# Two more PSUM banks for the last projection panel, and a group's elementwise work moved from GpSimd to VectorE and ScalarE

## The reference, cut to what matters

```python
xbc = silu(causal_depthwise_conv(xbc, conv_w, conv_b))     # 4 taps along the sequence, on x, B and C
y = ssd_chunked_scan(xs * dt, dt * a, bm, cm)              # a scan over chunks, state carried
y = y + d_skip * xs
y = y * silu(z)                                            # the gating
y = rmsnorm(y, norm_g)                                     # needs the sum of y*y over all groups
x = x + y @ w_out
```

## Time and profile before

| | |
|---|---|
| median of 3 runs | 2429.52 us (2429.28 to 2430.1) |
| span of the profiled execution | 2427.2 us |
| the profiled execution's time outside its span | not recorded |
| PE busy | 2237.2 us (92%) |
| DVE busy | 1369.1 us (56%) |
| ACT busy | 709.5 us (29%) |
| POOL busy | 215.7 us (9%) |
| mean granted TensorE clock | 0.961 of full speed |

### The profile page before, as it was taken

How to read it: one execution, slowest core, us unless ns; L and a number is a source line. 1 busy time by engine, 2 the same in 40 slices (tenths; PEclk the granted TensorE clock), 3 DMA queues, 4 the chain that set the end, 5 groups by cost and what they waited for, 6 DMA issues and landing times.

```text
span 2427.2 us, 27940 instructions
## 1 busy us (share of the span) xinstructions
PE 2237.2 (92%) x9790; PEld 1764.4 (73%) x9790; DVE 1369.1 (56%) x2135; ACT 709.5 (29%) x907; POOL 215.7 (9%) x196
## 2 busy tenths in 40 slices
PE   4999989898998989899889999799999987887999
PEld 3888778686876867687678888678877766564887
DVE  4466766767676676767863323352257773445333
ACT  4222122222212222221433212252234453433211
POOL 0000301102030120203000000000000101111000
PEclk9999999999999999999999999999999998988999
DMA  4645454453545445353444323613332221100432
GB/s 139 199 142 168 122 162 143 133 157 113 162 128 153 140 139 148 124 157 127 165 159 159 124 95 130 214 56 95 94 90 82 84 66 52 37 7 22 143 129 86
DMA packets 213887, 294.19 MB, mean 121 GB/s; under 512 B 16122, under 2 KB 150162, under 8 KB 212690
## 3 DMA queue, kind: packets, MB, share of 16 engines
q1 hardware_dynamic: 200946, 256.18, 33.8%
q0 software_dynamic: 8624, 29.04, 4.6%
q10 hardware_dynamic: 4272, 8.39, 0.9%
HBM read 273.51 MB, written 20.05 MB: 121 GB/s over the span
## 4 chain that ended last, share of the span: by engine, by line
PE 82%; DVE 9%; issue 7%; ACT 1%; DMA 0%; POOL 0%; DVEq 0%; SPq 0%; ACTq 0%; POOLq 0%
PE ps L1878 24%; PE ps L1879 23%; PE ps L1880 23%; PE ps L1948 2%; DVE w_lo L1186 2%; PE ps L2145 1%; PE ps L1952 1%; DVE xst L1279 1%; PE ps L1955 1%; PE ps L2126 1%; DVE bct L1279 1%; PE ps L2124 1%; PE ps L1962 1%; PE ps L1939 1%; PE ps L2074 1%
## 5 line engine op out<-in xcount | busy, mean ns | idle before, releaser
L1878 PE MATMUL ps<-hn_hi,w_hi 128*128 128x512 f32 (+1 forms) x1296 | 538.2, 415 | 67.9 <-DVE gz L1298 45.4
L1880 PE MATMUL ps<-hn_hi,w_lo 128*128 128x512 f32 (+1 forms) x1296 | 518.4, 400 | 0.0
L1879 PE MATMUL ps<-hn_lo,w_hi 128*128 128x512 f32 (+1 forms) x1296 | 518.3, 400 | 0.0
L1414 DVE TENSOR_TENSOR w_lo<-w_raw,w_hi 128x1024 fp32r<-128x1024 f32 x178 | 217.7, 1224 | 531.8 <-ACT w_hi L945 530.5
L1186 DVE TENSOR_TENSOR w_lo<-w_raw,w_hi 128x1024 fp32r<-128x1024 f32 (+1 forms) x166 | 206.5, 1246 | 302.6 <-ACT w_hi L858 301.8
L945 ACT ACTIVATE w_hi<-w_raw 128x1024 fp32r<-128x1024 f32 x178 | 188.4, 1059 | 550.6 <-PE ps L1880 523.0
L1878 PEld LDWEIGHTS ps<-hn_hi,w_hi 128*128 128x128 f32 (+1 forms) x1296 | 247.1, 191 | 139.7 <-DVE w_lo L1186 76.4
L858 ACT ACTIVATE w_hi<-w_raw 128x1024 fp32r<-128x1024 f32 (+1 forms) x166 | 172.5, 1041 | 542.1 <-PE ps L1880 535.0
L1878 PE MATMUL ps<-w_hi,y_hi 128*128 128x512 f32 x768 | 307.1, 400 | 9.1 <-DVE y_lo L1423 6.1
L1879 PE MATMUL ps<-w_lo,y_hi 128*128 128x512 f32 x768 | 305.7, 398 | 0.0
L1880 PE MATMUL ps<-w_hi,y_lo 128*128 128x512 f32 x768 | 305.6, 398 | 0.0
(11 more groups left out here) (323 smaller groups left out, 2416.0 us busy)
## 6 DMA issues: line engine op xcount, KB each, us to landing
ada_raw<-in_w_ada_dram SPq DMA_DIRECT2D x128, 384.0 KB, 3.4
w_raw<-in_ssm_w_in_dram SPq DMA_DIRECT2D x96, 512.0 KB, 4.5
w_raw<-in_ssm_w_in_dram SPq DMA_DIRECT2D x128, 256.0 KB, 3.5
w_raw<-in_w_in_dram SPq DMA_DIRECT2D x64, 512.0 KB, 3.8
w_raw<-in_ssm_w_out_dram SPq DMA_DIRECT2D x60, 512.0 KB, 3.7
csb<-cs_rows POOLq DMA_DIRECT2D x32, 512.0 KB, 5.9
w_raw<-in_w_out_dram SPq DMA_DIRECT2D x32, 512.0 KB, 5.5
y_rows<-yt POOLq DMA_DIRECT2D x8, 1024.0 KB, 4.7
```

The lines of the kernel that those rows point to most:

```text
L1414: nc.vector.tensor_tensor(w_lo[:, slot, :], w_raw[:, slot, :], w_hi[:, slot, :].bitcast(F32), ALU.subtract).then_inc(lo_ready, 1)
L1878: nc.tensor.matmul(out_, a_hi, b_hi, start=start, stop=False)
L1879: nc.tensor.matmul(out_, a_hi, b_lo, start=False, stop=False)
L1880: return nc.tensor.matmul(out_, a_lo, b_hi, start=False, stop=stop)
```

## The change

- Panel 4 goes to banks 6 and 7, and its gate is taken in one piece. PE now waits, at u = 16, until the scan has left these banks (`y_chunk_skipped`); at u = 0 for the copy of panel 2, made at u = 13; at u = 4 for the gate of panel 3; and, ahead of the scan's first `chunk_sum`, for the gate of panel 4.
- DVE multiplies each chunk by `gz` right behind `chunk_skip` (five instructions there now, four before). POOL does no arithmetic in the groups, and stores `yt` ahead of `ada_part`.
- The first tap of each convolution is an ACT instruction (`conv_tap`, six for each group), the six others stay on DVE.
- ACT squares the gated chunk (`y_squares`, u = 17, three instructions into the scan's free buffers), DVE adds them up (`y_add`, four instructions at u = 18 and 19, in two sums `ysq` and `ysq_b`).
- The convolutions start one step earlier (u = 14, 16, 17), their constants at u = 12, and `ada_rows` take the steps of `ADA_SLOTS`, with its loads one step later on SP.
- Some semaphores of the second block are merged; no wait changes there.

```diff
+Z_BANK = (2, 6)
+ADA_SLOTS = (*range(1, 14), 15, 18, 19)
@@ SP
-                    k = u - AHEAD
+                    k = u - AHEAD - ADA_SLOTS[0]
@@ POOL
+                if prev:
+                    pool.wait_ge(yt_ready, gp * NQ + NQ)
+                    pool.dma_start(y_rows[bass.ds(gp * GB * P, GB * P), :].rearrange("(b p) n -> p b n", p=P),
+                                   yt[:]).then_inc(y_stored, 16)
...
-                        nc.gpsimd.tensor_tensor(yt[:], yt[:], gz[:], ALU.mult).then_inc(gated, 1)
...
-                        st.done(nc.gpsimd.tensor_tensor(ytmp[:], yt[:, b, :], yt[:, b, :], ALU.mult))
-                        st.wait()
-                        st.done(nc.gpsimd.tensor_tensor(ysq[:], ysq[:], ytmp[:], ALU.add))
@@ ACT
+            def conv_tap(g, j):
+                first = isinstance(g, int) and g == 0
+                if j == 0:
+                    act.wait_ge(gconv_ready, g + 1)
+                    if not first:
+                        act.wait_ge(chunk_summed, g * NQ)
+                elif not first:
+                    act.wait_ge(y_chunk_skipped, g * NQ)
+                act.wait_ge(x_acc_freed, g * 3 + j + 1)
+                for b in range(2):
+                    dst = bct[:, b, :] if j == 0 else xst[:, 2 * j - 2 + b, :]
+                    ins = nc.scalar.activation(dst, xraw[:, 2 * j + b, 3:3 + SEQ], ACT.Identity,
+                                               bias=gconv[:, 4, 2 * j + b:2 * j + b + 1],
+                                               scale=gconv[:, 3, 2 * j + b:2 * j + b + 1])
+                ins.then_inc(tap_ready, 1)
...
+            def y_squares(gq):
+                act.wait_ge(yt_ready, gq * NQ + NQ)
+                act.wait_ge(chunk_summed, gq * NQ + NQ)
+                nc.scalar.activation(seg[:].rearrange("p r q -> p (r q)"),
+                                     yt[:, 0:2, :].rearrange("p b n -> p (b n)"), ACT.Square
+                                     ).then_inc(y_part_squared, 1)
+                for b, to in ((2, xdt), (3, xw)):
+                    nc.scalar.activation(to[:].rearrange("p r d -> p (r d)"), yt[:, b, :], ACT.Square
+                                         ).then_inc(y_part_squared, 1)
...
-                    if cur and u in (5, 10, 14):
-                        take_raw(g, {5: 0, 10: 1, 14: 2}[u])
+                    if cur and u in (5, 10, 13):
+                        take_raw(g, {5: 0, 10: 1, 13: 2}[u])
+                    if cur and u == 15:
+                        conv_tanh(g, 0)
+                    if cur and u in (13, 15, 16):
+                        conv_tap(g, {13: 0, 15: 1, 16: 2}[u])
@@ DVE
-                ins.then_inc(yt_ready, 1)
+                ins.then_inc(y_chunk_skipped, 1)
+                dve.wait_ge(y_chunk_skipped, gp * NQ + c + 1)
+                nc.vector.tensor_tensor(yt[:, :, c * Q:(c + 1) * Q], yt[:, :, c * Q:(c + 1) * Q],
+                                        gz[:, :, c * Q:(c + 1) * Q], ALU.mult).then_inc(yt_ready, 1)
@@ PE
-                    if p == 0:
-                        if not isinstance(g, int) or g:
-                            pe.wait_ge(z_acc_freed, g * 3 - 1)
-                    elif p >= 2:
+                    later = not isinstance(g, int) or g > 0
+                    if p in (2, 3):
                         pe.wait_ge(x_acc_freed, g * 3 + p - 1)
+                    elif p == 0 and later:
+                        pe.wait_ge(x_acc_freed, g * 3)
+                    elif p == 1 and later:
+                        pe.wait_ge(z_acc_freed, g * 2 - 1)
+                    elif p == 4 and later:
+                        pe.wait_ge(y_chunk_skipped, g * NQ)
...
+                bank = Z_BANK[1] if p == 4 else 2 * (p % 2)
```

More of the change, by code:

```diff
@@ L741, in _ @@
             load_cs(0, 1)
+            st.done(nc.gpsimd.memset(ysq_b[:], 0.0))
+            st.wait()
             pool.sem_inc(yt_free, 1)
@@ L898, in z_tanh @@
                 act.wait_ge(conv_done, g * 3 + 2 + j)
[L899 to L909, removed]
+                act.wait_ge(unit_used, g * GU + (4 + j) * UPP + DT_UNITS)
+                b = Z_BANK[j]
+                nc.scalar.activation(th[:, 1 - j, :, :], ps[:, b:b + 2, :], ACT.Tanh, scale=0.5
+                                     ).then_inc(z_tanh_ready, 1)
+            def y_squares(gq):
[7 more added lines that the diff above has]
+                                         ).then_inc(y_part_squared, 1)
             def chunk_exps(gp, c):
@@ L1268, in conv @@
             def conv(g, j):
-                dve.wait_ge(x_acc_freed, g * 3 + j + 1)
+                dve.wait_ge(tap_ready, g * 3 + j + 1)
                 dst = [bct[:, b, :] if j == 0 else xst[:, 2 * j - 2 + b, :] for b in range(2)]
[L1272 to L1275, removed]
                 for k in (2, 1, 0):
                     for b in range(2):
-                        st.wait(1)
+                        if k < 2:
+                            st.wait(1)
                         tap = nc.vector.scalar_tensor_tensor(
@@ L1293, in z_silu, with y_add @@
             def z_silu(g, j):
[L1295 to L1300, removed]
-                dve.wait_ge(z_tanh_ready, g * 3 + 1)
-                if j == 0 and (not isinstance(g, int) or g):
-                    dve.wait_ge(gated, g)
-                b = 2 * (1 - j)
+                dve.wait_ge(z_tanh_ready, g * 2 + j + 1)
+                b = Z_BANK[j]
                 nc.vector.scalar_tensor_tensor(gz[:, 2 * j:2 * j + 2, :], th[:, 1 - j, :, :], 1.0,
                                                ps[:, b:b + 2, :], ALU.add, ALU.mult).then_inc(z_acc_freed, 1)
+            def y_add(gq, half):
+                parts = ([seg[:, 0:4, :].rearrange("p r q -> p (r q)"), seg[:, 4:8, :].rearrange("p r q -> p (r q)")],
+                         [xdt[:].rearrange("p r d -> p (r d)"), xw[:].rearrange("p r d -> p (r d)")])[half]
+                dve.wait_ge(y_part_squared, gq * 3 + (3 if half else 1))
+                if half:
+                    st.wait()
+                for acc, part in zip((ysq, ysq_b), parts):
+                    st.done(nc.vector.tensor_tensor(acc[:], acc[:], part, ALU.add))
             def chunk_prepare(gp, c):
@@ L1946, in chunk_sum @@
                 pe.wait_ge(chunk_mid, gp * NQ + c + 1)
+                if c == 0:
+                    pe.wait_ge(z_acc_freed, gp * 2 + 2)
                 for r in range(HPG):
```

90 lines of the change are left out of this document (41 added, 49 removed).

## The result

| | before | after |
|---|---|---|
| median | 2429.68 us (4 runs, 2429.28 to 2430.1) | 2339.24 us (4 runs, 2336.92 to 2339.84) |
| span of the profiled execution | 2427.2 us | 2338.1 us |
| mean granted clock | 0.961 | 0.972 |

The ratio is 0.9625, with a 95% interval of 0.9613 to 0.9637: the change makes the kernel faster by 90.4 us. The forecast was 2337.5 us, in a range of 2330 to 2352.

A forecast was written before the change was run, and what follows sets the result against it. PE's own sequence and its waits for late DVE at group boundaries were taken as the bound. Gains 86.6 + 5.1 + 1.0 - 0.7 = 92.0; 2427.2 - 92.0 + 2.3 = 2337.5 us, range 2330 to 2352.

The forecast's parts named there:

- end of the projection: Seven wait-free groups from 170.14 us: the projection ends at 1073.9 instead of 1160.5 us, a gain of 86.6 us.
- hand-over: PE's gap from the projection to the output projection: 4.0 us instead of 9.1, a gain of 5.1 us.
- half clock behind it: Low-clock stretch after the hand-over wait: 1 us gained back, between 0 and 2.6.
- fourth chunk gate: In the last group's scan, DVE's fourth chunk gate delays `y_hi`: a loss of 0.7 us.
- P = 129.1: Period in us of one group without PE waits: 117.9 for 18 units and the scan, plus 11.2 for two units.
- Rival 1: A PE wait stays in each group's tail, some 4.6 us in each of seven groups: 2370 us, chance 0.07.
- The banks at unit 16: Tightest link: DVE's last skip frees banks 6 and 7 at 414.9, PE wants them at 419.1; 4.2 us to spare.
- DVE's list: DVE's queued work around a group boundary, followed on group 2's times: through at 438.6, PE ends unit 19 at 441.5.
- POOL's interference: POOL's arithmetic slows DVE's first convolution: eight taps take 14.1 us instead of about 5.1, so 9.0 us removed.
- Rival 2: PE's clock does not stay up in the groups, falling at bank changes: 60 us given back, 2397 us, chance 0.03.
- Rival 3: SP's queue: late ada rows hold up weight loads, making the kernel slower, 2437 us, chance 0.02.
- Rival 4: The change does nothing, as DVE's total work is what PE waits for: 2429 us, chance 0.02.

The follow-up runs named there:

- run 5: The changed kernel with POOL's gating multiplication and squares put back, new banks and spread convolutions kept: 2345.03 us.
- run 6: The changed kernel with the spreading undone (all taps on DVE at steps 15 to 17, ada rows at 0 to 15): 2338.03 us.
- run 9: The changed kernel with the hand-over reordered: first y chunk rounded before the last tanh, its low part before the last gate, banks 0 to 3 handed over earlier: 2332.84 us.
- run 10: As run 9, and POOL also releases the space for `y_in` ahead of its last ada row: 2333.55 us.
- run 2: The kernel before with only POOL's arithmetic moved off (gating by chunk and adds on DVE, squares on ACT): 2365.44 us.
- run 4: The changed kernel with the banks undone (panel 4 in banks 0 and 1 again, its gate in halves): 2338.86 us.
- run 7: The changed kernel with five extra DVE delay instructions behind the first convolution in groups 1 to 7: 2342.67 us.
- run 8: The changed kernel with twelve extra DVE delay instructions behind the first convolution in groups 1 to 7: 2381.59 us.

## Why the prediction was right, point by point

| term | predicted | measured on the spans |
|---|---|---|
| end of the projection | 1160.5 to 1073.9: 86.6 | 1160.5 to 1075.1: 85.4 |
| hand-over | 5.1 | 9.1 to 4.25: 4.85 |
| half clock behind it | +1.0 | -0.5 |
| fourth chunk gate | -0.7 | -0.7 |
| the rest | 0 | 0.1 |
| sum | 92.0 | 89.1 = 2427.2 - 2338.1 |

- **P = 129.1** was exact, and the clock held 1.00 over the 899 us of the window. This was the term that mattered, and the wait-free stretch of the earlier trace rows gave it without a model of what DVE does. Rival 1 failed: no wait stays in a tail. What it described happens to the banks alone, with 2375.7 us against its 2370.
- **The banks at unit 16.** Free at 402.9, wanted at 407.1: 4.2 us, as predicted, and shown by the two delays. DVE arrived 0.47 us early, not 0.9; two ACT taps took 1.52 us, not 1.42.
- **DVE's list** ends at 425.9, where the prediction's 438.6 less the shift of 12.0 gives 426.6; the gate of panel 4 is done at 432.06, where it gives 431.8.
- **POOL's interference** was the cause of DVE's slow taps: 4.06 us for six without POOL's arithmetic, up to 10.15 with it in the same code. The Trainium skill (SBUF — State Buffer, on the shared port pair) has a DVE instruction with two SBUF inputs locked out for the whole of a GpSimd one that reads SBUF. The trace of run 5 agrees: the `w_lo` begun at 405.04 ended at 409.14, 1.09 us behind POOL's multiplication, where 1.22 is its usual time. The row that the prediction named for this rule, the 5.29 us of the first tap, is no instance of it, for that instruction reads one tensor only (`xraw`); it was held up as long all the same, and took 1.01 without POOL's arithmetic.
- **Rival 2** failed. PE went through all its banks in each group, and the clock was 1.00 over the 899 us. The second failure mode of the Trainium skill (TensorE: Matmul & The Clock Gate) did not show with matmuls that follow each other without a gap.
- **Rival 3**: SP's queue cost nothing, for no `w_lo` or `w_hi` was late. A neighbour of it was real, in `y_in`'s path at the end: PE's wait there was 8.36 us with POOL back and 4.16 with five delays, against 3.31.
- **Rival 4** (nothing changes, since DVE's total work is the bound) failed with the result: DVE is idle for 3.42 us at the very point where it was late.
- **Mis-sized**: the half clock. I counted 1 us back; it cost 0.5 more than before (from the first matmul of the output projection to the next wait 17.59 us, before 17.07). The start of group 1 was taken as unchanged, and it came 1.2 us later (the first turn of its scan at 182.57, before at 181.35): the low clock at the start of group 0 lasted 6.8 us, not 3.4, behind the same 2.63 us wait. The two together are 2.7 of the 2.9 us between 92.0 and 89.1. The 2.3 us that I put outside the span were 1.1 between that span and the median, which took back part of it.

What the prediction left unsaid is that its parts overlap. Its own slacks hinted at that: the gate of panel 4, done at 443.8, was next asked for near 464. With 20 us of slack by the banks, and 11 for `w_lo`, POOL's 9 us could have stayed.

## What to carry to other kernels

When one engine is late at a fixed point, find a stretch of the profile in which nobody waits, and price the change by its period; then check every new dependency by the times in the rows. When a change has several parts, each aimed at the same lateness, their gains don't add: two of three gave all of it here, or all but 6 us where POOL kept its work, and the third can be left out, or its work put where it is cheapest. Once the large waits are gone, look at the hand-overs and there also at what stands ahead of a release in a queue: ordering the first rounding ahead of the last gate took 1.8 us from a wait and 2.7 from the clock behind it.

## What the runs showed of the hardware that was not expected

- The low-clock stretch behind the same wait has two lengths. In all kernels PE waits for 2.63 us at the start of group 0. From 54 to 61.5 us the clock was 0.77 in five of the thirteen kernels and 0.54 to 0.61 in the rest, which is a stretch of about 3.4 or 6.8 us and up to 1.7 us of time. The first row is from the kernel before, the second from the changed one.

```profile
54.00:61.50 7.50, 6.07 (x21) 0.77 0.25 71
54.00:61.50 7.50, 6.33 (x15) 0.54 0.58 193
```

The single times of one kernel are 2331.83, 2331.85, 2333.55, 2333.72 and 2336.6 us. Steps of this kind could be the same thing, but only one execution of each kernel was profiled, so that is not shown.

- What follows the last scan takes another time in each kernel, though the code is all but the same. From the end of the wait that ends at 1153.79 in the changed kernel to the end of the span are 1184.3 us there, 1184.4 in the kernel before, 1182.9 to 1184.0 in runs 6, 9 and 10 and 1186.2 to 1187.1 in runs 2, 4, 7 and 8. So a difference of up to 4 us between two of these kernels says nothing about an edit until the trace shows where it lies.
- A short wait may leave the clock alone, and its length alone does not tell. Waits of 0.78 to 1.55 us within the output projection and at the hand-over left it at 1.00. With the banks alone, a wait of 1.85 us at 297.24 left it at 1.00 too, and one of 1.85 at 431.26 was followed by 0.63. The 3.31, 3.96 and 4.14 us waits were followed by 0.50 to 0.53. But at the hand-over a wait of 2.21 us (run 4) was followed by 0.52, and one of 2.83 (run 2) left the clock at 1.00. That a hand-over wait of 1.55 us cost only itself here, while one of 3.31 cost 2.7 us more, is a large part of what made run 9 gain so much.
